# Both directions of a recurrence level in one product over mixed keys

## What is computed

```python
def diff_attention(...):
    s = einsum('bqhmd,bkhmd->bhmqk', q, k); a = softmax(s)
    w = a[:, :, 0] - lam * a[:, :, 1]
    o = einsum('bhqk,bkhe->bqhe', w, v)
    return rmsnorm(o, subln_g) * (1 - lambda_init)

def hgrn2_bidirectional(...):            # 4 heads, key and value width 128
    log_f = log(lb + (1 - lb) * sigmoid(z)); k_in = (1 - lb) * sigmoid(-z)
    # z: forward, and backward on the reversed sequence
    new_state = exp(sum log_f) * state + k_dec^T v
    o = rmsnorm(o_forward + o_backward, norm_g) * silu(g)
```

## Time and profile before

| | us |
|---|---|
| median of the runs shown (3) | 967.99 |
| lowest, highest | 966.05, 968.95 |
| the profiled execution | 976.23 |
| its span, first to last instruction | 974.4 |
| TensorE busy in it | 936.3 |
| VectorE, ScalarE, GpSimd busy | 599.4, 480.6, 117.7 |

### The profile page before, as it was taken

The page is one execution under the profiler, slowest core; times in us unless marked ns, Lnnn a source line. Parts: engine busy times, 40 slices in busy tenths (PEclk is TensorE's granted clock), DMA queues, the critical chain, the costliest instruction groups (busy, mean ns, idle before and its releaser), DMA issues.

```text
span 974.4 us, 14431 instructions
## 1 busy us (share of the span) xinstructions
PE 936.3 (96%) x4981; PEld 789.7 (81%) x4981; DVE 599.4 (62%) x897; ACT 480.6 (49%) x707; POOL 117.7 (12%) x107
## 2 busy tenths in 40 slices
PE   6999999999999999999999999899989999999986
PEld 5788888888777778788888877688867999999965
DVE  5655455578646535655455557878776775766764
ACT  6544444465745435544444457323555454545463
POOL 5210000020123202000000021532202000000020
PEclk9999999999979779999999999999999999999998
DMA  9796667447512213756565537342224756565511
GB/s 312 205 271 200 201 199 218 137 147 234 200 66 79 74 43 106 224 188 190 179 191 194 176 105 237 121 138 87 67 86 151 228 176 194 171 202 183 186 52 44
DMA packets 122041, 157.44 MB, mean 162 GB/s; under 512 B 10047, under 2 KB 83011, under 8 KB 122000
## 3 DMA queue, kind: packets, MB, share of 16 engines
q1 hardware_dynamic: 119648, 151.65, 48.7%
q0 software_dynamic: 1904, 4.65, 1.9%
q10 hardware_dynamic: 448, 0.59, 0.2%
HBM read 155.79 MB, written 1.07 MB: 161 GB/s over the span
## 4 chain that ended last, share of the span: by engine, by line
PE 85%; DVE 7%; ACT 4%; issue 2%; POOL 1%; SPq 1%; DMA 1%; DVEq 0%; ACTq 0%; POOLq 0%
PE bank L469 21%; PE bank L471 20%; PE bank L470 20%; PE bank L499 4%; PE bank L501 4%; PE bank L500 4%; DVE w_lo L1612 2%; PE bank L1025 2%; ACT w_hi L1160 1%; PE bank L852 1%; PE bank L581 1%; PE bank L850 1%; PE bank L682 1%; PE bank L860 1%; SPq L374 1%
## 5 line engine op out<-in xcount | busy, mean ns | idle before, releaser
L1619 DVE TENSOR_TENSOR w_lo<-w_raw,w_hi 128x1024 fp32r<-128x1024 f32 x180 | 220.2, 1224 | 177.4 <-ACT w_hi L1169 177.4
L1169 ACT ACTIVATE w_hi<-w_raw 128x1024 fp32r<-128x1024 f32 x180 | 190.4, 1058 | 210.8 <-PE bank L471 174.1
L469 PE MATMUL bank<-w_hi,x_hi 128*128 128x512 f32 (+1 forms) x688 | 278.8, 405 | 7.1 <-DVE hb L1668 2.5
L471 PE MATMUL bank<-w_hi,x_lo 128*128 128x512 f32 (+1 forms) x688 | 270.0, 392 | 0.0
L470 PE MATMUL bank<-w_lo,x_hi 128*128 128x512 f32 (+1 forms) x688 | 269.7, 392 | 0.0
L469 PEld LDWEIGHTS bank<-w_hi,x_hi 128*128 128x128 f32 x688 | 130.9, 190 | 43.3 <-issue 11.0
L471 PEld LDWEIGHTS bank<-w_hi,x_lo 128*128 128x128 f32 x688 | 131.0, 190 | 28.2
L470 PEld LDWEIGHTS bank<-w_lo,x_hi 128*128 128x128 f32 x688 | 131.4, 191 | 24.1
L1612 DVE TENSOR_TENSOR w_lo<-w_raw,w_hi 128x1024 fp32r<-128x1024 f32 x97 | 120.3, 1266 | 49.2 <-ACT w_hi L1160 48.6
L1160 ACT ACTIVATE w_hi<-w_raw 128x1024 fp32r<-128x1024 f32 x108 | 112.1, 1055 | 55.2 <-PE bank L471 50.9
L469 PE MATMUL bank<-w_hi,h_hi 128*128 128x512 f32 (+1 forms) x304 | 116.1, 382 | 4.9 <-DVE h_lo L1778 2.5
(11 more groups left out here) (291 smaller groups left out, 956.7 us busy)
## 6 DMA issues: line engine op xcount, KB each, us to landing
w_raw<-in_w_ffn_gate SPq DMA_DIRECT2D x132, 256.0 KB, 2.9
w_raw<-in_w_ffn_up SPq DMA_DIRECT2D x132, 256.0 KB, 3.1
w_raw<-in_w_ffn_down SPq DMA_DIRECT2D x132, 256.0 KB, 3.0
w_raw<-in_w_in SPq DMA_DIRECT2D x104, 256.0 KB, 3.1
w_raw<-in_w_out SPq DMA_DIRECT2D x32, 256.0 KB, 3.4
w_raw<-in_w_ple_gate SPq DMA_DIRECT2D x16, 256.0 KB, 3.4
arena<-bias_rows POOLq DMA_DIRECT2D x8, 256.0 KB, 4.3
w_raw<-in_cmp_w_k SPq DMA_DIRECT2D x8, 256.0 KB, 4.7
```

Of the source, the lines that this page charges most:

```text
L469: pe.matmul(out_, hi, wh, start=start, stop=False)
L471: return pe.matmul(out_, lo, wh, start=False, stop=stop)
L1169: act.activation(whi[:, slot * UNIT:(slot + 1) * UNIT], raw[:, slot * UNIT:(slot + 1) * UNIT], ACT.Copy).then_inc(sem("hi_done"), 1)
L1619: dve.tensor_tensor(wlo[:, s_], raw[:, s_], whi[:, s_].bitcast(F32), ALU.subtract).then_inc(sem("lo_done"), 1)
```

## The change

It has six parts. (1) ScalarE writes, for each level and pair, a tile `KMIX` of mixed keys (`key_mix`): of each group of 2h tokens the first run from the forward keys and the second from the backward keys. TensorE then does both directions in one product with 128 columns of queries, read by the same pattern out of the two halves of `HQ` (`both_ways`), four products for a level and pair in place of eight. (2) ScalarE copies levels 0 and 8 (`same_place`, `across`) and the rotated tiles (`turned2`); VectorE no longer does. (3) GpSimd's growth waits for the key copy, `kmix_done`, and not for the product; VectorE grows keys and queries with fewer waits, and at h = 64 only the half of the elements that level 8 still uses. (4) The transposes of column group 3 go from behind (4,2) and (4,3) to behind (5,0) and (5,1). (5) `da_weights` leaves the first map unscaled: the second map is weighted by lambda times the ratio of the two denominators and added in one operation for each tile; the common factor falls out in the norm, whose epsilon is scaled by the squared denominators (`DEPS`). (6) Waits follow from these.

```diff
@@ tables @@
+        KMIX = (DV, DV + 512)
-        T2_FIRST = {0: 0, 1: 2, 2: 4, 3: 6, 4: 8}
+        T2_AT = {(1, 2): (0, 0), (1, 3): (1, 0), (2, 2): (2, 1), (2, 3): (3, 1), (3, 2): (4, 2), (3, 3): (5, 2),
+                 (5, 0): (6, 3), (5, 1): (7, 3), (5, 2): (8, 4), (5, 3): (9, 4)}
+        def both_ways(off, n, h):
+
+            return raw_ap(arena, ARENA, off, [[2 * h, n // (2 * h)], [1024 + h, 2], [1, h]])
         def grown(base, pr, h):
+            if h == 64:
+                return raw_ap(arena, ARENA, base + pr * 512, [[1024 + h + P, 2], [S, 2], [1, h]])
             return raw_ap(arena, ARENA, base + pr * 512, [[1024 + h, 2], [2 * h, 256 // h], [1, h]])
@@ TensorE, level(n) @@
-                    if pr == 1:
-                        pe.wait_ge(sem("grown_pool"), L - 1)
-                if L >= 1:
-                    pe.wait_ge(sem("at_done"), n - 1)
+                if 1 <= L <= 7:
+                    pe.wait_ge(sem("kmix_done"), n - 1)
...
+                if L == 1:
+                    pe.wait_ge(sem("at0_done"), pr + 1)
+                elif L >= 2:
+                    pe.wait_ge(sem("at_done"), n - 3)
...
-                            for z, o in ((0, h), (1, 0)):
-                                mm = pe.matmul(halves_of(b, 512, c + o, h), av(HK + 1024 * z + at, [P]),
-                                               halves_of(arena, ARENA, HQ + 1024 * (1 - z) + at + o, h),
-                                               start=True, stop=True)
+                            mm = pe.matmul(b[:, c:c + P], av(KMIX[pr] + hh * S + blk * P, [P]), both_ways(HQ + at, P, h),
+                                           start=True, stop=True)
@@ ScalarE @@
+            def key_mix(n):
+                L, pr = divmod(n, 2)
+                if not 1 <= L <= 7:
+                    return
+                if L == 1:
+                    act.wait_ge(sem("k_done"), 8)
+                else:
+                    act.wait_ge(sem("grown_pool") if pr else sem("grown_k"), L - 1)
+                    act.wait_ge(sem("lv_full"), n - 1)
+                h = 1 << (L - 1)
+                act.activation(av(KMIX[pr], [256 // h, 2, h]), both_ways(HK + pr * 512, 512, h), ACT.Copy
+                               ).then_inc(sem("kmix_done"), 1)
...
             for p in range(8):
                 for j in range(4):
+                    if (p, j) == (4, 3):
+                        same_place(0)
+                        same_place(1)
+                    for n in levels_at(p, j):
+                        key_mix(n)
                     if j == 3:
                         staged2(p)
...
                     split(U_IN2 + 4 * p + j + RING)
@@ VectorE, level(n) and da_weights(h) @@
+                if pr == 0:
...
+                    dve.wait_ge(sem("kmix_done"), n - 1)
+                    dve.tensor_tensor(grown(HK, 0, h), grown(HK, 0, h), growth(0, h, True), ALU.mult
+                                      ).then_inc(sem("grown_k"), 1)
                 dve.wait_ge(sem("lv_full"), n + 1)
...
-                for m in range(M):
-                    e1 = av(DE + 512 + m * S, [S])
-                    dve.tensor_scalar(e1, e1, sm(DRC + 4 * h + 2 + m), None, ALU.mult).then_inc(sem("e1_done"), 1)
...
+                    dve.scalar_tensor_tensor(av(DW + m * S, [S]), av(DE + 512 + m * S, [S]), sm(DRC + 4 * h + 2 + m),
+                                             av(DE + m * S, [S]), ALU.mult, ALU.add).then_inc(sem("dw_done"), 1)
@@ GpSimd, grow(L) @@
-                pool.wait_ge(sem("lv_full"), 2 * L + 2)
+                pool.wait_ge(sem("kmix_done"), 2 * L)
```

More of the change, by code:

```diff
@@ L297, in levels_at @@
             return (8 + 2 * k, 9 + 2 * k) if k < 5 else ()
-        def halves_of(tensor, row, off, h):
-            return raw_ap(tensor, row, off, [[2 * h, 64 // h], [1, h]])
+        def both_ways(off, n, h):
+            return raw_ap(arena, ARENA, off, [[2 * h, n // (2 * h)], [1024 + h, 2], [1, h]])
         def grown(base, pr, h):
+            if h == 64:
+                return raw_ap(arena, ARENA, base + pr * 512, [[1024 + h + P, 2], [S, 2], [1, h]])
             return raw_ap(arena, ARENA, base + pr * 512, [[1024 + h, 2], [2 * h, 256 // h], [1, h]])
@@ L310, in growth @@
             nb = 1024 // h
-            if keys:
-                return raw_ap(tensor, row, off + nb + pr * 512 // h + 1, [[-(nb + 1), 2], [2, 256 // h], [0, h]])
-            return raw_ap(tensor, row, off + pr * 512 // h + 1, [[nb - 1, 2], [2, 256 // h], [0, h]])
+            o, step = (nb, -(nb + 1)) if keys else (0, nb - 1)
+            if h == 64:
+                return raw_ap(tensor, row, off + o + pr * 512 // h + 1, [[step + 2, 2], [4, 2], [0, h]])
+            return raw_ap(tensor, row, off + o + pr * 512 // h + 1, [[step, 2], [2, 256 // h], [0, h]])
         def bias_of(h, n):
@@ L1096, in _ @@
                     k_unit(u % RING, j, BANKS2[p])
-                    if j >= 2 and p - 1 in T2_FIRST:
-                        tgroup2(T2_FIRST[p - 1] + j - 2, p - 1)
+                    if (p, j) in T2_AT:
+                        tgroup2(*T2_AT[p, j])
                     for n in levels_at(p, j):
@@ L1536, in _ @@
                     split(U_IN2 + 4 * p + j + RING)
-                    if j >= 2 and p in (2, 3):
-                        sigmoids(2 * (p - 1) + j - 2)
+                    if p in (2, 3, 5) and (p, j) in T2_AT:
+                        g = T2_AT[p, j][0]
+                        sigmoids(g) if p < 5 else turned2(g)
                     if p >= 6:
                         k = 4 * (p - 6) + j
+                        if k == 4:
+                            across(0)
+                            across(1)
                         if k in (0, 2, 4):
@@ new lines, in level @@
+                h = 1 << (L - 1)
+                if n == 2:
+                    dve.wait_ge(sem("hq_init"), 1)
+                    dve.wait_ge(sem("t_prod"), 6)
+                    dve.wait_ge(sem("k_done"), 8)
+                    dve.wait_ge(sem("con3_in"), 16)
+                if pr == 0:
+                    if L >= 2:
+                        dve.wait_ge(sem("grown_k"), L - 1)
+                    dve.wait_ge(sem("kmix_done"), n - 1)
+                    dve.tensor_tensor(grown(HK, 0, h), grown(HK, 0, h), growth(0, h, True), ALU.mult
+                                      ).then_inc(sem("grown_k"), 1)
@@ new lines, in level @@
+                dve.wait_ge(sem("lv_full"), n + 1)
+                if L >= 2:
+                    dve.wait_ge(sem("grown_dve"), 2 * (L - 2) + pr + 1)
+                dve.tensor_tensor(grown(HQ, pr, h), grown(HQ, pr, h), growth(pr, h, False), ALU.mult
+                                  ).then_inc(sem("grown_dve"), 1)
+                if L == 1:
+                    dve.wait_ge(sem("at0_done"), pr + 1)
+                else:
+                    dve.wait_ge(sem("at_done"), n - 3)
+                dve.copy_predicated(raw_ap(arena, ARENA, AT + pr * 1024, [[512, 2], [384, 2], [1, P]]),
+                                    raw_ap(con, C_ALL, C_LEVEL + (L - 1) * P, [[0, 2], [0, 2], [1, P]]).bitcast(I32),
+                                    bank[4 + pr][:, :].rearrange("p (a b c) -> p a b c", a=2, b=2)
@@ L2298, in quad_sums @@
                 dve.wait_ge(sem("qss_done"), 2 * k + 2)
-                dve.tensor_scalar(sm(QMS + 8 * k, 8), sm(QSS + 8 * k, 8), 1.0 / P, EPS, ALU.mult, ALU.add
-                                  ).then_inc(sem("qms_done"), 1)
+                if k:
+                    dve.wait_ge(sem("deps_done"), 1)
+                    dve.scalar_tensor_tensor(sm(QMS + 8, 8), sm(QSS + 8, 8), 1.0 / P, sm(DEPS, 8), ALU.mult, ALU.add
+                                             ).then_inc(sem("qms_done"), 1)
+                else:
+                    dve.tensor_scalar(sm(QMS, 8), sm(QSS, 8), 1.0 / P, EPS, ALU.mult, ALU.add
+                                      ).then_inc(sem("qms_done"), 1)
                 dve.wait_ge(sem("qms_done"), 2 * k + 1)
@@ L2350, in _ @@
                     split(U_IN2 + 4 * p + j + RING)
-                    if j >= 2 and p in (1, 4, 5):
-                        turned2(T2_FIRST[p - 1] + j - 2)
-                    if j >= 2 and p in (2, 3):
-                        forget(2 * (p - 1) + j - 2)
+                    if p < 4 and (p, j) in T2_AT:
+                        g = T2_AT[p, j][0]
+                        turned2(g) if p == 1 else forget(g)
                     if (p, j) == (3, 3):
```

64 lines of the change are left out of this document (28 added, 36 removed).

## The result

| | before | after |
|---|---|---|
| median (6 runs of each), us | 967.24 | 960.71 |
| lowest to highest | 966.05 to 968.95 | 959.25 to 963.68 |
| profiled execution / its span | 976.23 / 974.4 | 959.75 / 957.9 |

The ratio of after to before is 0.994, 95% interval 0.9922 to 0.9957: the changed kernel is 6.5 us faster. The forecast was 958.5, in a range of 954.5 to 964.0.

What follows compares the result with a forecast made beforehand. TensorE was taken as just barely the bound, with VectorE's loop between heads' maxima deciding the gain behind 668 us. Terms summed to 10.0 us, less 0.5 gives 9.5, from 967.99 to 958.5; range 954.5 to 964.0.

Steps and rivals of the forecast that it cites:

- Level products: Recurrence levels on TensorE: 224 passes of 64 columns become 112 of 128 at 0.110 us each, saving 12.3 us of work.
- Key copies: ScalarE gets 14 copies of 512 columns, taken at 0.60 us each (0.50 start to start), far bound 1.9.
- First stretch: Up to the start of unit (5,0): 634.5 against 640.38, 5.9 us earlier, with 1.0 added for GpSimd contention.
- Second stretch: Units of projection 5 up to VectorE's first maxima: reached at 660.0 against 668.23, 8.2 us earlier.
- Clock: TensorE's granted clock expected at 1.00 throughout the changed stretch; renewed falls were left to a rival with chance 0.18.
- The walk: Step-by-step timing of the changed stretch; gave 10.0 us won, cut to 9.5 because its version of before ended 0.5 early.
- the rival's own prices: Clock falls again: 1.6 us before (5,0) or level 7, hidden before level 5; one fall 960.1, two 961.7; chance 0.18.
- Round 2: VectorE's loop from the second head's maxima to the third's: 10.83 us against 12.36 before.
- The third rival: GpSimd holds VectorE for whole instructions, 0.98 in place of 0.33 in four loop levels: 2.6 us more, 961.1; chance 0.10.
- Round 3: Last round between maxima, set by TensorE with unit, 32 output passes, turn, unit: 10.63 us against 10.47 before.
- Weighting: VectorE's weighting in the loop: 1.27 us, now 1.80, as two scalings go; in the first round nearly eaten by later weight half.
- Sum: Whole changed stretch: 8.2 + 0.15 + 1.5 - 0.15 + 0.3 = 10.0 us, less 0.5, so 9.5 won.

Runs made afterwards that it cites:

- e1: Changed kernel with twelve unread 512-column matmuls in front of each wait before levels 5 and 7; 957.87 us, ratio 0.9922 to the kernel before.
- e11: e1 with GpSimd's two products of gate and gain held back until the scores of head 2 are made; 956.59 us, ratio 0.9919 to before.
- e7: Changed kernel with two scalings of the second map put back ahead of the weighting's sums; 958.91 us, ratio 0.9919 to the kernel before.
- e0: Changed kernel run again with nothing altered; 959.38 us, ratio 0.9927 to the kernel before.
- e10: Kernel before the change, run again unaltered; median 966.03 us.
- e2: Changed kernel with ScalarE's key copies of levels 5 and 7 ahead of the previous head's exponentials; 956.22 us, ratio 0.9878 to the kernel before.
- e6: e5 with VectorE's first-pair key growth of levels 5 and 7 moved into its wait for the exponentials; 953.72 us, ratio 0.9868 to before.
- e8: e6 with eight unread 512-column matmuls in front of the level pair at (6,2); 955.00 us, ratio 0.9892 to the kernel before.
- e3: Changed kernel with column group 3's transposes back behind units (4,2) and (4,3); 964.14 us, ratio 0.998 to the kernel before.
- e4: Changed kernel with every level product of levels 1 to 7 done twice; 963.97 us, ratio 0.9972 to the kernel before.
- e5: e2 with the turns of heads 0 and 1 moved behind units (6,2) and (7,0); 958.00 us, ratio 0.9897 to the kernel before.

## Why the prediction was right in the time and wrong in its middle

- **Level products**: right. 112 passes, 0.10 to 0.12 from start to start at full clock; no second pass for the second run.
- **Key copies**: nearly right, 0.675 on average where 0.60 was taken, 0.52 from start to start in the loop.
- **First stretch**: unit (5,0) starts 14.31 behind `hg_prepare`, forecast 13.7. The contention with GpSimd was 5.04 - 3.79 = 1.25 on the three halves, taken as 1.0.
- **Second stretch**: 7.6 us earlier at the first maxima, forecast 8.2.
- **Clock**: the step that failed. The forecast took the clock as 1.00 throughout. Its own list of waits had 3.3 and 3.1 us, both above the 2.54 that had left the clock alone, and still it gave the falls 0.18. The 2.54 was no safe length either: the same wait is followed by a fall in after and in nine more profiles (below). The price was wrong as well: "before level 5 VectorE's loop hides it" is refuted by e1, where that round loses 1.64. The walk had 0.31 us of wait for the second high half of the round, and at full clock there are 0.52 (e1); it didn't ask what a fall does to the unit that frees the slot, and with the fall the wait is 2.17. The falls came before levels 5 and 7 and not before (5,0). By the rival's own prices, nothing for level 5, that is its case of one fall, 960.1, and 960.71 was measured; that these are so close is luck, since it prices the two falls at 1.6 where they cost 3.3.
- **Round 2**: besides a fall, 1.2 us for GpSimd holding VectorE (e11). The third rival had the mechanism, but looked only at growths; it was the two gate products behind the last growth. They stood in the trace of before too, beside a weight half that took 1.55 and copies out of PSUM; the change moved them onto a growth. The remaining 0.5 (11.37 against 10.83) is TensorE's own chain of level 7, turn, unit, level 8 and scores, which in e11 runs without a wait; the walk had left it open for 0.50 only.
- **Round 3**: the four terms printed for it add up to 9.56; with the scores, 1.07 from start to start, which it does not name, they give the 10.63. Measured 10.79.
- **Weighting**: the forecast said that a later weight half nearly eats it; e7 shows that in rounds 1 and 3 it is worth nothing, and in the tail 0.40.
- **Sum**: in the stretch 9.5 forecast, 4.6 measured. The missing 4.9 are 3.3 clock, 1.2 GpSimd, 0.6 the first maxima, less 0.2 for the rest.

**The time is in part luck.** In the stretch, which is all that the forecast worked out, the gain is half of what it said. The medians differ by 6.5 us, by 7.5 in e0 and by 6.2 between e10 and all runs of after, the stretch by 4.6: the rest, some 2 to 3 us, was won where no line of the change stands, and that brought the time near the forecast.

**Open** is why. The profiles show where executions differ outside the stretch: in falls of the clock. Ahead of it, the product of `hg_prepare` starts at 606.3 in the two profiles without a fall there (e7, e11), at 608.2 in those with one, at 331 us (after, e0, e2, e10), and at 609.0 to 611.2 in those with two or a longer one (the others, but for the first profile of before). Behind it, the fall behind the wait of 2.54 comes in some profiles only. The runs of before (962.9 to 968.3 in e10) lie above its profiled execution for the most part, with a lower mean clock (0.986 to 0.990 against 0.993), so they had more falls than it; why before should have more of them than after, or whether it does, no run here shows.

## What to carry to other kernels

Work taken off the bounding engine turns into waits, and a wait of two or three microseconds on TensorE can cost half as much again in the clock behind it (1.64 behind 2.83, 0.9 to 1.1 behind 2.06): list the waits that a change opens, and price each as wait plus fall wherever another engine waits for that stretch. A small copy belongs ahead of the long block of the same engine if its input is ready then (e2 won 3.5 us in the stretch by that alone). When a loop has several limits close together, look at what the next engine starts once the first is eased: here GpSimd's products moved onto VectorE's growth.

## What the runs showed of the hardware

- A fall isn't a matter of the wait's length alone. One and the same wait of 2.54, at 906 to 929 us, left the clock at 1.00 in four profiles (before, e10, e6, e8) and was followed by 0.50 in the ten others. Behind 2.06 before (5,0) the clock stayed at 1.00 in four profiles and fell in three (e7, e8, e11), at about 1.0 us each; at 2.83 it fell seven times of eight; behind 4.29 always (three). e2 had a fall behind 1.64 and none behind 1.88.
- Two short waits in a row can do it too. In the tail TensorE waits 1.18 and soon after 1.01; in six of the twelve profiles other than those of before (e2, e3, e4, e5, e7 with 1.58 and 0.78, e11) the clock fell there, and the tail took 19.8 to 20.3 us in place of 18.9 to 19.0. Behind the single waits of 1.03 in e4 it didn't.
- The Trainium skill, "TensorE: Matmul & The Clock Gate", section "Part 1: The HAM clock gate", says of the slow matmuls at a kernel's start that their number varies from run to run of one kernel. That the same wait brings a fall in one profile and none in the next agrees with this.
- A copy of 512 columns on ScalarE, SBUF to SBUF, takes 0.86 us with runs of one element, 0.70 with runs of two and 0.62 to 0.64 with longer ones: short runs cost up to two fifths more, far from the 1.9 at which the change would have broken even.
- Two gate products of GpSimd take 3.51 us beside VectorE's half and growth (1.59 and 1.50, e1) and 2.54 away from them (e11): there both sides pay. In e6 they took 2.54 beside a growth that took 1.54: there VectorE alone paid.
